# A mixture-of-experts kernel: gather and token table one round ahead, the last round written out, GpSimd drains replaced by waits

## What is computed

```python
logits = ht @ w_router + b_router
top_val, top_idx = lax.top_k(logits, 4)
gates = softmax(top_val)
# for each expert e, on the tokens that chose it:
gu = xb @ w_gate_up[e] + b_gate_up[e]            # 1024 -> 2048
x_glu, x_lin = minimum(gu[:, :1024], 7), clip(gu[:, 1024:], -7, 7)
act = x_glu * sigmoid(1.702 * x_glu) * (x_lin + 1)
y = act @ w_down[e] + b_down[e]                  # 1024 -> 1024
out[token] += gate * y
# then a final RMS norm
```

## Time and profile before

| | us |
|---|---|
| three runs, median | 1603.59 |
| lowest and highest | 1598.92, 1614.74 |
| the profiled execution | 1607.89 |
| its span, first to last instruction | 1606.1 |
| the expert loops in it, from the first to the last L1499 that stands in a loop (30 rounds) | 387.51 to 1550.57 |
| granted clock of PE, mean share of full speed | 0.966 |

### The profile page before, as it was taken

One profiled execution on the slowest core, in us unless ns is written; L12 is line 12 of the kernel. 1 busy time (PEld: TensorE's weight loads), 2 busy tenths in 40 slices (PEclk: granted clock), 3 DMA queues, 4 the chain that ended last, 5 costly groups with the idle time before them and its releaser, 6 DMA issues.

```text
span 1606.1 us, 20095 instructions
## 1 busy us (share of the span) xinstructions
PE 1485.2 (92%) x6780; PEld 1208.3 (75%) x6780; DVE 1221.3 (76%) x936; ACT 985.1 (61%) x723; POOL 529.5 (33%) x413
## 2 busy tenths in 40 slices
PE   6989989679899999999999999999999999999994
PEld 5867877558787787787777888778778877787773
DVE  5444444477798787888877888788887887887884
ACT  4243241456677676776766777677776776776773
POOL 0000000433343353453333444344343443343341
PEclk9999999779999999999999999999999999999997
DMA  8212322577899999999989999899998999899973
GB/s 296 79 59 76 103 83 66 180 253 278 302 352 344 317 349 323 350 351 329 342 306 317 348 357 355 303 352 357 347 349 316 358 355 349 309 349 325 344 261 111
DMA packets 128616, 453.66 MB, mean 282 GB/s; under 512 B 13455, under 2 KB 13471, under 8 KB 128400
## 3 DMA queue, kind: packets, MB, share of 16 engines
q1 hardware_dynamic: 116832, 432.04, 75.0%
q0 software_dynamic: 9984, 18.47, 4.6%
q10 hardware_dynamic: 1776, 2.83, 0.6%
HBM read 447.84 MB, written 23.07 MB: 293 GB/s over the span
## 4 chain that ended last, share of the span: by engine, by line
PE 62%; DMA 15%; issue 10%; POOLq 4%; ACT 4%; DVE 3%; POOL 2%; ACTq 0%; SPq 0%; DVEq 0%
DMA xg<-h_rows,idx_gather 14%; PE ps L1521 14%; PE ps L1522 13%; PE ps L1527 13%; PE ps L1255 4%; PE ps L1261 4%; PE ps L1256 4%; PE ps L1499 2%; POOLq L521 2%; ACT actT_hi L750 2%; PE ps L1508 2%; POOL tab L522 2%; POOLq L530 1%; PE ps L1513 1%; DVE wlo L860 1%
## 5 line engine op out<-in xcount | busy, mean ns | idle before, releaser
L860 DVE TENSOR_TENSOR wlo<-raw,whi 128x2048 fp32r<-128x2048 f32 x274 | 624.3, 2291 | 151.6 <-ACT whi L617 151.5
L617 ACT ACTIVATE whi<-raw 128x2048 fp32r<-128x2048 f32 x274 | 525.4, 1917 | 208.5 <-PE ps L1527 167.2
L1521 PE MATMUL ps<-whi,xT_hi 128*128 128x512 f32 x1024 | 409.8, 400 | 0.0
L1522 PE MATMUL ps<-whi,xT_lo 128*128 128x512 f32 x1024 | 403.0, 394 | 0.0
L1527 PE MATMUL ps<-wlo,xT_hi 128*128 128x512 f32 x1024 | 279.4, 394 | 0.0
L1521 PEld LDWEIGHTS ps<-whi,xT_hi 128*128 128x128 f32 x1024 | 193.7, 189 | 45.9
L1527 PEld LDWEIGHTS ps<-wlo,xT_hi 128*128 128x128 f32 x1024 | 193.1, 189 | 44.9
L860 DVE TENSOR_TENSOR wlo<-raw_a,whi 128x2048 fp32r<-128x2048 f32 x64 | 147.0, 2296 | 103.4 <-ACT whi L617 103.4
L1522 PEld LDWEIGHTS ps<-whi,xT_lo 128*128 128x128 f32 x1024 | 193.8, 189 | 41.7
L1521 PE MATMUL ps<-whi,actT_hi 128*128 128x512 f32 x512 | 214.2, 418 | 4.3 <-issue 4.3
L1522 PE MATMUL ps<-whi,actT_lo 128*128 128x512 f32 x512 | 210.0, 410 | 0.0
(11 more groups left out here) (212 smaller groups left out, 1608.2 us busy)
## 6 DMA issues: line engine op xcount, KB each, us to landing
raw<-in_w_gate_up SPq DMA_DIRECT2D x130, 1024.0 KB, 7.1
raw<-in_w_down SPq DMA_DIRECT2D x126, 1024.0 KB, 8.1
raw_a<-in_w_gate_up SPq DMA_DIRECT2D x63, 1024.0 KB, 6.7
raw_b<-in_w_gate_up SPq DMA_DIRECT2D x63, 1024.0 KB, 6.7
raw<-in_w_in SPq DMA_DIRECT2D x14, 1024.0 KB, 5.1
raw<-in_w_out SPq DMA_DIRECT2D x4, 1024.0 KB, 5.0
x<-in_x SPq DMA_DIRECT2D x4, 512.0 KB, 8.1
acc_rows<-x SPq DMA_DIRECT2D x4, 512.0 KB, 2.6
```

The costliest lines, as they stand in the source:

```text
L617: nc.scalar.activation(whi_slot(n), raw_slot(slot_of(n)), ACT.Copy).then_inc(hi_done, 1)
L860: nc.vector.tensor_tensor(wlo_slot(n), raw_slot(slot_of(n)), whi_slot(n).bitcast(F32), ALU.subtract).then_inc(lo_done, 1)
L1521: mm(ps[:, bank + half, :], x_hi_t[:, k0 + k, :], w_hi_ap, start=k0 + k == 0 and not started, stop=False)
L1522: mm(ps[:, bank + half, :], x_lo_t[:, k0 + k, :], w_hi_ap, start=False, stop=False)
```

## The change

Three parts, in one diff:

- **One round ahead.** PE's table product in a round is for expert i+3 instead of i+2. POOL stores the table of expert i+3 and finds the slots of expert i+4; its gather of expert i+3 now stands after `select`, behind a wait for the tokens of expert i+2 (which frees `xg`). The first expert's `gate_up` takes the table product of expert 2, and POOL does table 2, slots 3 and gather 2 ahead of its loop.
- **Last round written out.** The loops have 30 rounds. The last is straight code: no table and no tokens in it, the features of expert 31 go between the second and third down unit of expert 30 and their split into `xT_hi` and `xT_lo`; the buffers of the down bias move to where `xg` and `actT_lo` lay, and its three loads are issued within the round.
- **Waits for drains.** The instruction that has to be finished raises a semaphore of its own; `finished` waits for that count and raises a semaphore `order`.

The rows read back from `acc_rows` also use the semaphores `x_in` again, instead of four of their own.

```diff
-            def find_slots(e, numbers, done):
-                nc.gpsimd.tensor_copy(pair[:, :, 0:4], pairs[...])
-                pl.drain()
+            def finished(of, count):
+                pl.wait_ge(of, count)
+                pl.sem_inc(order, 1)
+
+            def find_slots(e, numbers, done, count):
+                nc.gpsimd.tensor_copy(pair[:, :, 0:4], pairs[...]).then_inc(pair_copied, 1)
+                finished(pair_copied, count)
...
-            with pl.Fori(0, E - 1) as i:
-                pl.wait_ge(x_tr, i + 2)
-                pl.wait_ge(gathered, i * 16 + 32)
-                pl.wait_ge(tab_raw, i + 3)
-                store_table(expert_rows(i + 2), tab_s)
-                gather(expert_rows(i + 2), gathered)
-                find_slots(i + 3, slots[:, 0:P], has_s)
+            with pl.Fori(0, E - 2) as i:
+                pl.wait_ge(tab_raw, i + 4)
+                store_table(expert_rows(i + 3), tab_s, i + 4)
+                find_slots(i + 4, slots[:, 0:P], has_s, i + 3)
                 pl.wait_ge(used, i * U_E + (U_LOOP + U_GU))
                 select(sel_gu, i + 2).then_inc(sel_gu_s, 1)
+                pl.wait_ge(tab_s, i + 4)
+                pl.wait_ge(x_tr, i + 3)
+                finished(gathered, i * 16 + 48)
+                gather(expert_rows(i + 3), gathered, i + 4)
                 pl.wait_ge(y_s, i + 2)
-                pl.wait_ge(scattered, i * 16 + 16)
-                scatter(expert_rows(i), scattered)
-            pl.wait_ge(x_lo, E + 1)
+                finished(scattered, i * 16 + 16)
+                scatter(expert_rows(i), scattered, i + 2)
+            pl.wait_ge(y_s, E)
+            pl.wait_ge(scattered, 16 * (E - 1))
+            scatter(expert_rows(E - 2), scattered, E)
+            pl.wait_ge(used, U_ALL - U_DN)
             nc.gpsimd.memset(bdn[3 * E:P, :].bitcast(F32), 0.0).then_inc(bdn_zero, 1)
...
                     if u == 2 and e > 0:
                         features(e - 1, i)
                         pe.wait_ge(lin_s, i + e)
-                        table(e + 1, i)
+                    if u == 2 and more:
+                        table(e + 2, i)
...
-            with pe.Fori(0, E - 1) as i:
+            with pe.Fori(0, E - 2) as i:
                 gate_up(U_LOOP, 1, i)
                 tokens(2, i)
-                down(U_LOOP + U_GU, 0, i)
-            features(E - 1)
+                down_units(U_LOOP + U_GU, 0, range(U_DN), i)
+            gate_up(U_LOOP, 1, E - 2, more=False)
+            down_units(U_ALL - 2 * U_DN, E - 2, (0, 1))
+            features(E - 1, last_one=True)
+            down_units(U_ALL - 2 * U_DN, E - 2, (2, 3))
...
-            down(U_ALL - U_DN, E - 1)
+            down_units(U_ALL - U_DN, E - 1, range(U_DN), 0, xT_hi, xT_lo)
```

More of the change, by code:

```diff
@@ L340, in build @@
     fin_g_in = sem("final_gain_in")
-    x1_out, x_back = sem("residual_stored"), [sem(f"rows_back{c}") for c in range(NC)]
+    x1_out = sem("residual_stored")
     has_tr, hasT_s, yhi_s, ylo_s, f_ps = (sem("slots_transposed"), sem("hasT_ready"), sem("last_y_hi"), sem("last_y_lo"),
@@ L516, in find_slots, with store_table @@
                 last.then_inc(done, 1)
-            def store_table(rows, done):
-                nc.gpsimd.tensor_tensor(rows, slot_sums[:, :], cst[:, C_OFF:C_OFF + 4], ALU.add)
-                pl.drain()
+            def store_table(rows, done, count):
+                nc.gpsimd.tensor_tensor(rows, slot_sums[:, :], cst[:, C_OFF:C_OFF + 4], ALU.add).then_inc(table_moved, 1)
+                finished(table_moved, count)
                 nc.gpsimd.tensor_tensor(rows[:, 1:2], rows[:, 1:2], rows[:, 2:3], ALU.add).then_inc(done, 1)
@@ L525, in expert_rows, with gather @@
                 return tab[:, bass.ds(e, 1), :].rearrange("p e f -> p (e f)")
-            def gather(rows, done):
-                nc.gpsimd.tensor_copy(idx_gather[:, 0:1], rows[:, 0:1])
-                pl.drain()
+            def gather(rows, done, count):
+                nc.gpsimd.tensor_copy(idx_gather[:, 0:1], rows[:, 0:1]).then_inc(gather_index, 1)
+                finished(gather_index, count)
                 pl.indirect_dma_start(out=xg[:, :], out_offset=None, in_=h_rows,
@@ L533, in gather, with scatter @@
                                       bounds_check=S - 1, oob_is_err=False).then_inc(done, 16)
-            def scatter(rows, done):
-                nc.gpsimd.tensor_copy(idx_scatter[:, 0:1], rows[:, 0:1])
-                pl.drain()
+            def scatter(rows, done, count):
+                nc.gpsimd.tensor_copy(idx_scatter[:, 0:1], rows[:, 0:1]).then_inc(scatter_index, 1)
+                finished(scatter_index, count)
                 scatter_rows(y[:, :], done)
@@ L601, in _ @@
                         select(sel_gu, e).then_inc(v_sel, 1)
[L602 to L603 removed]
+                        nc.gpsimd.tensor_copy(slot_row[:, :], slots[:, bass.ds(first, P)]).then_inc(slot_row_s, 1)
+                        finished(slot_row_s, i + 1)
+                        find_slots(e, slot_row[:, :], v_has, i + (E + 1))
                         pl.wait_ge(v_raw, i + 1)
[L605 to L606 removed]
+                        store_table(tab_over[:, :], v_tab, i + (E + 2))
+                        finished(v_tab, i + 1)
+                        gather(tab_over[:, :], v_gather, i + (E + 2))
                         pl.wait_ge(v_add, i * NC + NC)
@@ L775, in _ @@
             act_e.wait_ge(hn_out, 16 * NC)
-            for n in (21, 22, 23, 24, 25):
+            for n in (21, 22, 23):
+                hi(n)
+            copy_table(2)
+            for n in (24, 25):
                 hi(n)
@@ L793, in _ @@
                 features_hi(0, i)
[L794 removed]
+                copy_table(3, i)
                 hi(32, i)
@@ L804, in _ @@
                 hi(41, i)
-            act_e.wait_ge(x_lo, E + 1)
+            i = E - 2
+            hi(30, i)
+            hi(31, i)
+            features_hi(E - 2)
+            hi(32, i)
+            hi(33, i)
+            sigmoid(1, i)
+            act_e.wait_ge(x_tr, E)
+            act_e.wait_ge(gathered, 16 * (E + 1))
             for r in (0, E, 2 * E):
                 act_e.dma_start(bdn_raw[r:r + E, :], b_down[0]).then_inc(bdn_in, 16)
-            features_hi(E - 1)
+            for n in (34, 35, 36, 37, 38):
+                hi(n, i)
+            features_hi(E - 1, 0, xT_hi)
+            for n in (39, 40):
+                hi(n, i)
+            gated_rows(E - 2, 16 * (E - 1), U_ALL - U_DN)
+            hi(41, i)
             act_e.wait_ge(gate_tr, 1)
@@ L1171, in _ @@
                 lo(41, i)
-            features_lo(E - 1)
+            i = E - 2
+            lo(30, i)
+            lo(31, i)
+            features_lo(E - 2)
+            lo(32, i)
+            lo(33, i)
+            lo(34, i)
+            gate_glu(1, i)
+            lo(35, i)
+            lo(36, i)
+            lo(37, i)
+            clamp_lin(1, i)
+            activated(1, i)
+            lo(38, i)
+            features_lo(E - 1, 0, xT_hi, xT_lo)
+            lo(39, i)
+            lo(40, i)
+            lo(41, i)
             v.wait_ge(gateT_hi, 1)
@@ L1500, in tokens, with features @@
                 last.then_inc(x_tr, 1)
-            def features(e, i=0):
+            def features(e, i=0, last_one=False):
                 pe.wait_ge(act_s, i + (e + 1))
-                pe.wait_ge(x_hi, i + (e + 2))
-                pe.wait_ge(x_lo, i + (e + 2))
+                if last_one:
+                    pe.wait_ge(aT_hi, e)
+                    pe.wait_ge(aT_lo, e)
+                else:
+                    pe.wait_ge(x_hi, i + (e + 2))
+                    pe.wait_ge(x_lo, i + (e + 2))
                 for j in range(KD):
@@ L1551, in gate_up, with down_units @@
                     unit_matmuls(n0 + u, i, KM * (u % 4), 2 * (u // 4), xT_hi, xT_lo, True)
-            def down(n0, e, i=0):
+            def down_units(n0, e, units, i=0, a_hi=actT_hi, a_lo=actT_lo):
                 pe.wait_ge(aT_hi, i + (e + 1))
@@ L1556, in down @@
                 pe.wait_ge(y_s, i + (e + 1))
-                for u in range(U_DN):
-                    unit_matmuls(n0 + u, i, KM * u, 4, actT_hi, actT_lo, False)
+                for u in units:
+                    unit_matmuls(n0 + u, i, KM * u, 4, a_hi, a_lo, False)
             table(0)
```

60 lines of the change are left out of this document (36 added, 24 removed).

## The result

The changed kernel took 1532.79 us (median of 4 runs, 1531.35 to 1533.77), the kernel before 1602.01 beside it (4 runs, 1598.92 to 1614.74): 0.9553 of the time, 95% interval 0.9500 to 0.9606. The forecast was 1537.0, in a range from 1528 to 1560. The profiled execution took 1533.77 us, its span 1532.0, against 1607.89 and 1606.1: 74.1 us less.

The account below looks back on a forecast made before the run. PE's work and POOL's path to the late gather were taken to bound the loops by turns. 64.5 + 6.4 = 70.9 us off the profiled 1607.89 gave 1537 us, range 1528 to 1560.

Parts of the forecast that it names:

- The bound: In the expert loops, PE's own work and a path through POOL ending in the gather take turns as bound.
- Part 1: Gather one round ahead in the expert loops: PE's wait and the half clock behind it disappear, -64.5 us.
- Part 2: Last round written out: 26.0 us instead of 32.4 from the eight units' end to the last rows, -6.4 us.
- Part 3: Waits for drains on POOL: 0 us, since gathering one round ahead already gives most of what they could give.
- The starting point: Sum taken from the profiled execution, 1607.89 us, 4.3 above the median; run differences put down to late gathers.
- The transfers become the bound: Rival in the loops: at 350 GB/s a round takes 37.4 us, the kernel 1561 us; chance 0.08.
- DVE has to wait: Rival in the loops: POOL's instructions block DVE, in the middle 41 us a round, 1669 us; chance 0.02.
- It doesn't do what it says: Rival: PE waits for something else in the new order, half of the 64.5 us stays, 1569 us; chance 0.05.

Follow-up runs that it names:

- the kernel with one drain put back: The kernel before with GpSimd's drains replaced by waits, except the drain between the two table instructions, which is there again: 1640.41 us, 1.0228 of before.

## Why the prediction was right, point by point

*The bound.* Right: two things took turns, and without the late gather PE alone is left. Wrong in one small thing: the round from 663.57 to 700.19, which I took as one "that waits for nothing". The timeline of PE's weight loads at its end, in the kernel before, has it otherwise, and I hadn't read it:

```profile
700.18 0.42 PEld L1499 LDWEIGHTS ps<-cst,xg 128*128 128x128 f32 x4 [0.35 <-DMA xg<-h_rows,idx_gather]
```

The round ended late for the gather too, by so little that the row of PE's busy time doesn't show it. A round that waits for nothing is 36.47 us, in the changed kernel and in four of the experiments.

*Part 1, 64.5 us.* Measured 69.3. This is the term that was mis-sized: 30 x 0.15 = 4.5 for the round, and 0.4 for the table product that the last round no longer has (36.02 us there), which I had set against the one more at the front. The 1.3 us by which the loops begin later are within what runs of the changed kernel differ by (spans of 1529.5 to 1532.0), so what the front paid can't be told. The gather's spare time, estimated at 17.7 us, is 23: I took off the 3.2 us of the issue and then a landing that already counts from the start of the issue, and POOL's two copies, 2.4 us each in my sum, took 1.51 and 0.18.

*Part 2, 6.4 us.* Measured 6.1; the 26.0 us of its sum are 26.2, the two waits of 1.2 and 0.6 are 1.26 and 0.53. The features' place is shown to be the greater part of it. The reads of SP cost nothing, as taken: they are issued at 1505.08, 7.35 us ahead of the first sum.

*Part 3, 0.* Right as a term beside part 1. The waits-only kernel shows why "the two are not to be added" had to be said: the waits could have given not "most" but all of the loops' gain. What I hadn't worked out is how little was missing. A round was late by 1.5 us on average (46.0 / 30), and the waits take 5.1 us off the path from table to gather (8.16 to 3.03). So the 64.5 us, which I gave to the round ahead, are no more its own than the waits': either brings them.

*The starting point.* Right: the sum was taken from one of the slower executions, on the ground that the spread comes from rounds late for their gather. The four runs of the changed kernel lie within 2.4 us, those of the kernel before within 15.8.

*The transfers become the bound.* They don't: 359 GB/s, with 374 to be had for nothing, and 385 to 386 as the most that the rounds reached. The Trainium skill, "DMA: Bandwidth & Descriptors", section "Measured (HBM→SBUF, 128 partitions, SWDGE, issued from GpSimd)", gives a core some 358 GB/s when both cores of its memory domain stream. The rounds run at just that number, and the runs with more bytes show that it isn't what holds them; what the neighbour does was varied in no run. Nor were the slices of 404 to 427 GB/s, which I held against it, a measure of whole rounds.

*DVE has to wait.* Hardly: its split takes 2.29 us in the changed kernel, in the loops 2.33 at most. POOL waits, and more than before: in the loops the median of one of the four instructions on `has` is 1.55 us, for 0.60, and nobody waits for it. "So far POOL does the waiting" was not the whole of it, though, as a row of the kernel with waits alone shows:

```profile
853.74 2.43 DVE L873 TENSOR_TENSOR wlo<-raw,whi 128x2048 fp32r<-128x2048 f32 x1 [0.95 <-ACT whi L630]
```

It stands in all 30 rounds: a split that starts 0.08 us behind an instruction on `has` takes 2.43 us, 0.14 more than the others, while that instruction runs on for 0.52. The Trainium skill, "SBUF — State Buffer", section "Who interferes with whom", blocks the one that starts second, whichever it is, to the end of the first. For POOL the traces agree: its short instructions that start in a split end 0.04 to 0.06 us behind it. DVE lost 0.14 us there, and not the 0.52.

*It doesn't do what it says.* No new name stands among those that PE waits for in the loops.

## What to carry to other kernels

Hold a cure against how late the path really is: 1.5 us a round was missing here, so one drain less took most of the loss, and the waits or the round ahead took all of it; such gains must not be added. A drain is paid by what stands behind it: over the kernel with waits alone, the drains that were left behind two short instructions cost 10 us, the one left ahead of them, with a wait between the two, 103. To find what an engine's round takes without waiting, read its loads as well, and don't take a round that is busy throughout for one that waits for nothing.

## What the runs showed of the hardware

- A drain on GpSimd waits for transfers that GpSimd issued before, though no instruction behind it needs them: in the kernel before, L522 starts 0.29 us after the landing of the scatter in all 30 rounds, and in the kernel with one drain put back L530 starts 0.42 to 0.44 us after it. With one taken out the next took the wait over (4.36 us, for 4.57); ahead of the gather in the kernel with drains and the round ahead, with no such transfer under way, it cost no more than a wait (0.86 us).
- A short GpSimd instruction (0.2 us: the second table instruction, the copies of row numbers and of pairs) that starts within one of DVE's weight splits takes up to 2.3 us. In the loops of the kernel before 74 start within one: 70 of them end 0.04 to 0.06 us behind its end, the other four start in its last 0.05 us and take 0.2. So 0.2 us of delay can decide: behind the drain of the table one of two short instructions met a split in 20 of 30 rounds, and in all 30 where the second stood 0.22 us later.
- The transfers of this core reached 385 to 386 GB/s over whole rounds. With 1.05 MB more the rounds kept their 36.5 us at that rate while ACT's waits for weights gathered, and only the end was later.
